# Pooling output projection: the twelve sums of weight blocks on GpSimd in place of VectorE

## The reference, cut to what matters

```python
def pooling_layer(x, g_norm, w_in, w_grp, b_grp, scale, w_out):
    ...
    mix = mix.reshape(B, S, POOL_WIDTH) * scale          # 256 x 4096
    return (mix * jax.nn.silu(z)) @ w_out                # w_out: 4096 x 2048
```

## Time and profile before

| | us |
|---|---|
| median of 3 runs | 2607.45 |
| lowest and highest | 2606.75, 2607.81 |
| the profiled execution's own time | 2608.36 |
| its span, first to last instruction | 2606.5 |
| TensorE busy, matmuls | 2590.2 (99%) |
| VectorE busy | 2058.8 (79%) |
| ScalarE busy | 1345.0 (52%) |
| GpSimd busy | 169.9 (7%) |

### The profile page before, as it was taken

The page is one execution under the profiler, slowest core; times in us unless marked ns, Lnnn a source line. Parts: engine busy times, 40 slices in busy tenths (PEclk is TensorE's granted clock), DMA queues, the critical chain, the costliest instruction groups (busy, mean ns, idle before and its releaser), DMA issues.

```text
span 2606.5 us, 35341 instructions
## 1 busy us (share of the span) xinstructions
PE 2590.2 (99%) x12626; PEld 2175.6 (83%) x12626; DVE 2058.8 (79%) x2881; ACT 1345.0 (52%) x1712; POOL 169.9 (7%) x332
## 2 busy tenths in 40 slices
PE   9999999999999999999999999999999999999998
PEld 7888888888888888888888888888888888788887
DVE  5887777776756868779877788987899899989565
ACT  5444444444444445444556555454656666574453
POOL 0000000000000000000002250432000000000000
PEclk9999999999999999999999999999999999999999
DMA  8555555555575565556565555645565565665754
GB/s 304 181 185 177 184 183 185 186 189 194 191 192 201 189 202 199 189 201 215 193 202 173 173 168 161 200 156 174 182 198 194 194 195 181 198 194 195 248 173 159
DMA packets 151494, 498.97 MB, mean 191 GB/s; under 512 B 28720, under 2 KB 29456, under 8 KB 150832
## 3 DMA queue, kind: packets, MB, share of 16 engines
q1 hardware_dynamic: 148736, 486.19, 56.4%
q0 software_dynamic: 2608, 10.74, 1.2%
HBM read 492.66 MB, written 4.21 MB: 191 GB/s over the span
## 4 chain that ended last, share of the span: by engine, by line
PE 97%; DVE 2%; ACT 1%; issue 0%; DMA 0%; POOL 0%; SPq 0%; DVEq 0%; ACTq 0%
PE PS L2246 23%; PE PS L2248 23%; PE PS L2247 23%; PE PS L2290 7%; PE PS L2269 5%; PE PS L2294 4%; PE PS L2274 2%; PE PS L2480 2%; PE PS L2461 2%; PE PS L2459 2%; PE PS L2460 2%; DVE yl L1938 1%; DVE wlo L1260 0%; PE PS L2487 0%; PE PS L2304 0%
## 5 line engine op out<-in xcount | busy, mean ns | idle before, releaser
L756 ACT CAST whi<-raw 128x1024 fp32r<-128x1024 f32 x887 | 928.0, 1050 | 1114.5 <-PE PS L2248 819.6
L1260 DVE TENSOR_TENSOR wlo<-raw,whi 128x1024 fp32r<-128x1024 f32 x887 | 1082.0, 1225 | 454.2 <-ACT whi L756 449.5
L2246 PE MATMUL PS<-whi,aHL 128*128 128x512 f32 x1904 | 744.7, 391 | 3.6 <-DVE wlo L1319 2.3
L2248 PE MATMUL PS<-whi,aHL 128*128 128x512 f32 x1904 | 741.1, 389 | 0.0
L2247 PE MATMUL PS<-wlo,aHL 128*128 128x512 f32 x1904 | 741.0, 389 | 0.0
L2246 PEld LDWEIGHTS PS<-whi,aHL 128*128 128x128 f32 x1904 | 357.5, 188 | 79.3 <-issue 2.7
L2248 PEld LDWEIGHTS PS<-whi,aHL 128*128 128x128 f32 x1904 | 357.4, 188 | 74.6
L2247 PEld LDWEIGHTS PS<-wlo,aHL 128*128 128x128 f32 x1904 | 357.6, 188 | 73.1
L2290 PE MATMUL PS<-aHL,whi 128*128 128x512 f32 x768 | 206.0, 400 | 1.7 <-DVE aHL L1296 1.4
L2290 PEld LDWEIGHTS PS<-aHL,whi 128*128 128x128 f32 x768 | 135.1, 190 | 24.5 <-DVE aHL L1296 1.6
L2269 PE MATMUL PS<-aHL,whi 128*128 128x512 f32 x512 | 128.2, 392 | 0.0
(11 more groups left out here) (395 smaller groups left out, 3112.3 us busy)
## 6 DMA issues: line engine op xcount, KB each, us to landing
raw<-in_stream SPq DMA_DIRECT2D x888, 512.0 KB, 3.3
quad<-in_stream SPq DMA_DIRECT2D x12, 512.0 KB, 5.6
xT<-in_xT SPq DMA_DIRECT2D x4, 512.0 KB, 6.7
H<-in_x SPq DMA_DIRECT2D x4, 512.0 KB, 8.5
pB<-in_pool_b POOLq DMA_DIRECT2D x4, 512.0 KB, 4.7
iT<-diag_in SPq DMA_DIRECT2D x16, 128.0 KB, 3.8
bg<-in_b_gate POOLq DMA_DIRECT2D x8, 256.0 KB, 3.8
out<-eb SPq DMA_DIRECT2D x8, 256.0 KB, 2.1
```

The costliest lines, as they stand in the source:

```text
L756: nc.scalar.copy(whi[:, s], raw[:, s]).then_inc(hi_done, 1 + blank)
L1260: nc.vector.tensor_tensor(wlo[:, s], raw[:, s], whi[:, s].bitcast(F32), ALU.subtract).then_inc(lo_done, 1 + blank)
L2246: mm(out, hi[:, kt + k, tok], whi[:, s, k], start=kt + k == 0, stop=False)
L2248: ins = mm(out, lo[:, kt + k, tok], whi[:, s, k], start=False, stop=last and k == KPC - 1)
```

## The change

The twelve sums are taken out of VectorE's `quad_lo` and made by GpSimd with the same operation on the same tiles, one group after the other, behind its two DMA issues. As the sum is no longer in the same queue as the low half that reads its place, GpSimd waits for that low half on `lo_done` (`low_taken`), and T3, which writes over 12, waits for T1, which reads it, and T4 for T2. SyncE gets one more wait: before it loads over the place of 21 it waits for the T4 sum, which reads 21.

```diff
@@ sync: loads of the next group @@
                     if w in ("T3", "22", "21", "T4") and g + 1 < len(PO_QUADS):
+                        if w == "21":
+                            sp.wait_ge(quad_add, added(g, "T4"))
                         sp.wait_ge(lo_done, q * RING + (RING + x - RING + 1))
                         quad_load(g + 1, {"T3": "11", "22": "12", "21": "22", "T4": "21"}[w])
@@ gpsimd @@
             pool.dma_start(pE[:], dram["pT"]).then_inc(row_in, 16)
+
+            def quad_sum(g, to, v):
+
+                loaded(pool, g, v)
+                nc.gpsimd.tensor_tensor(quad_at(g, to), quad_at(g, to), quad_at(g, v), ALU.add).then_inc(quad_add, 1)
+
+            def low_taken(g, w):
+
+                pool.wait_ge(lo_done, PO_AT + RING + PO_PLAN.index((g, w)) + 1)
+
+            for g in range(len(PO_QUADS)):
+                low_taken(g, "11")
+                quad_sum(g, "11", "12")
+                pool.wait_ge(quad_add, added(g, "T1"))
+                quad_sum(g, "12", "22")
+                low_taken(g, "T1")
+                quad_sum(g, "11", "22")
+                low_taken(g, "T2")
+                pool.wait_ge(quad_add, added(g, "T2"))
+                quad_sum(g, "11", "21")
             row_scale(M_FN)
@@ vector @@
-            def quad_sum(g, to, v, w):
-
-                loaded(dve, g, v)
-                nc.vector.tensor_tensor(quad_at(g, to), quad_at(g, to), quad_at(g, v), ALU.add).then_inc(quad_add, 1)
-
             def quad_lo(q, x, g, w):
...
-                if w == "11":
-                    quad_sum(g, "11", "12", "T1")
-                if w == "T1":
-                    dve.wait_ge(quad_add, added(g, "T1"))
-                    quad_sum(g, "12", "22", "T3")
-                    quad_sum(g, "11", "22", "T2")
-                if w == "T2":
-                    quad_sum(g, "11", "21", "T4")
```

## The result

| | before | after |
|---|---|---|
| median of 14 runs each, us | 2607.68 | 2612.08 |
| lowest and highest, us | 2606.75, 2608.71 | 2610.39, 2614.10 |
| profiled execution, own time, us | 2608.36 | 2610.59 |
| its span, us | 2606.5 | 2608.8 |

The change makes the kernel 4.4 us slower: ratio 1.0017, 95% interval 1.0009 to 1.0024. That is inside the 0.2% that was called no change, and clear of the measurement's own uncertainty. It lies within the stated range (2606.8 to 2614.5), 3.1 us above the likeliest time (2609.0), and just above the range given for that case alone (2607.5 to 2612).

What follows compares the result with a forecast made beforehand. TensorE, busy 2590.2 of 2606.5 us, was taken to bound the kernel. Gaps of 0.9 + 0.4 + 0.2 = 1.5 us in three groups, added to the median 2607.45, gave 2609.0 us, range 2606.8 to 2614.5.

Steps and rivals of the forecast that it cites:

- that case alone: Exclusion between GpSimd's sums and VectorE at 2.1 to 2.5 us: 2609.0 us, own range 2607.5 to 2612, chance 0.58.
- the relief: Twelve sums leaving VectorE free 13.6 us there, worth 0 us by itself since TensorE has no gap.
- exclusion in both directions: GpSimd's sums and VectorE's instructions with two SBUF inputs block each other; VectorE stands 2.0 us per sum where they meet.
- The replay: Step through three groups of sums and low halves, giving TensorE delays of 0.9, 0.4 and 0.2 us.
- the hold of a sum: One 1024-element sum on GpSimd takes 2.2 us: 0.2 start, 2.0 moving data and keeping VectorE out.
- the prediction's own rule: Three holds lie ahead of the first plain block after T2, so each extra 0.1 us costs 0.9 in all.
- the smallest margin: Block 21's low half in group 0 ends 1.4 us before TensorE asks for it, claimed as the least in hand.
- SyncE's loads: Quad loads at 1285.23 cost 0, at worst 1 us once; later by more than 2 us would show it wrong.
- The new wait: SyncE's wait for T4 before loading over block 21's place: cost 0, at worst 1 us once.
- No exclusion: Rival: the engines hardly exclude each other, VectorE's reads interleave and nothing starves; 2607.5 us, chance 0.20.
- The slow sum: Rival: a sum takes 3.3 us, delaying each group's first plain block after T2; 2618.9 us, chance 0.19.
- Faster: Rival: VectorE's freed 13.6 us let something start sooner; 2607 us at best, chance 0.03.

Runs made afterwards that it cites:

- e1: The twelve sums left out on any engine, products using unsummed blocks, against the kernel before: 2607.22 us, ratio 0.9999.
- f5: The change with only the three T4 sums on GpSimd, T1, T3 and T2 staying on VectorE: 2607.28 us, ratio 1.0000.
- e2: e1 plus twelve 128x1024 adds on GpSimd into unused tiles, which nobody waits for: 2611.31 us, ratio 1.0013.
- f8: The change once more, unaltered, for a second trace: 2611.25 us in one run.
- e3: e2 with three 128x1024 fills on GpSimd, which read nothing, in place of each add: 2607.62 us, ratio 1.0000.
- e4: The change with each sum made in two GpSimd instructions of 512 elements: 2609.80 us, ratio 1.0009.

## Why the prediction was right, and by how much it was off

**Right: the relief is worth nothing** (predicted 0; e1's window is the same to 0.01 us). TensorE was full, and VectorE's 13.6 us were cover, not path.

**Right: exclusion in both directions, and turns.** The replay named block 22 as the first victim, three holds deep, then block 26 by a little, block 44 behind the norm's row product, and group 2's first plain block, which is block 54. TensorE stopped before block 22, was 0.3 us late for block 26 and stopped before 44 and 54, and nowhere else in the stretch. That exclusion was taken from adds of 28 to 70 elements, and it held at 1024.

**Off: the size of one term, the hold of a sum.** I took 2.2 us for a sum, 2.0 of it on the port, from a slope over 8 to 76 elements. A sum that nobody delays takes 2.40 us (f5: mean 2401 ns), 0.2 of it start, so 2.2 on the port. This mis-sized term made the sum less than half of what came: 1.5 us forecast, 3.4 by the trace, 4.4 by the medians. By the prediction's own rule each 0.1 us costs 0.3 us a group, 0.9 in all: 1.5 + 2 x 0.9 = 3.3 us, and the trace has 3.4. That the total fits so well is partly luck. By groups the prediction had 0.9, 0.4 and 0.2, the corrected hold makes it 1.5, 1.0 and 0.8, and the trace has 1.8, 0.8 and 0.8, the last by a path that the replay did not have. The estimate halved from the Trainium skill (GPSIMD Engine Reference, section 3.1), 2.25 us, is hardly nearer than my 2.2, and short by 0.15.

**The third gap's path was not seen.** For group 2 the replay had block 54's low half between the sums T1 and T3, and took 0.2 us for a load that lands late. In the change T3's sum went first and the low half behind it. So the place was named for another reason than the one that came, which is luck. The reading that 1.4 us was the smallest margin was also wrong beyond group 0: before the change block 54's low half ended at 1297.73 and was asked for at 1298.58, 0.85 us in hand.

```profile
1296.50 1.23 DVE L1260 TENSOR_TENSOR wlo<-raw,whi 128x1024 fp32r<-128x1024 f32 x1 [2.38 <-ACT whi L756]
...
1298.58 0.39 PE L2459 MATMUL PS<-whi,oH 128*128 128x512 f32 x1
```

SyncE's loads were to come no more than 2 us later if the replay held, and they came 4.1 later. This sign against the prediction did show: 2.6 us of it are TensorE's delay, for which the replay had 1.3, and about 1.5 are T4's hold, which it did not carry on to the loads. The new wait itself cost 0, as said.

**Rivals.** No exclusion (0.20) is refuted by the low halves of 3.42 us and by e2. The slow sum (0.19) is not what happened: a sum alone takes 2.40 us, under the 2.6 that this rival asked for, and 3.44 only where it waits its turn. Faster (0.03) did not come.

**What stays open.** The delay by 1345 is 3.4 us, the medians differ by 4.4 (interval 2.3 to 6.3). The change's runs spread over 3.7 us, those of before over 2.0; its ten runs with a mean granted clock of 0.999 average 2611.6 us, the four with 0.997 or 0.998 2613.1. So part of the rest may go with the clock; where it dips in those runs no trace shows. The gap at 1371 that f8 has and the first trace has not adds another 0.7 us of scatter. What makes up the last 1.0 us of the 4.4 stays open. Whether VectorE's instructions with one input in PSUM are spared, as the replay assumed, was not tried: none of them met a sum.

## What to carry to other kernels

An add of two SBUF tiles that is moved from VectorE to GpSimd does not lie beside VectorE's instructions with two SBUF inputs: the move replaces 1.13 us of VectorE's time by a stop of up to 2.2. GpSimd work that only writes (e3) does lie beside them. Count the holds that can lie ahead of one urgent instruction, not the sums: three ahead of a plain block cost 1.3 us and more in group 0, two cost 0.3 us there and nothing in group 1, and one a group (f5) nothing. Look also at who is in the queue when a hold ends: where VectorE has nothing waiting, two sums run behind one another, and in group 2 the low half that came next stood behind the second. If the work must be moved, cut it up (which helped in two groups of three) or put it where no one is waiting, and look first whether VectorE is on the path at all.

## What the runs showed of the hardware that I had not expected

A recorded duration contains the wait for the other engine: one and the same 128x1024 subtraction shows 1.22, 1.73 and 3.42 us, one sum 2.40 and 3.44, and the idle time written beside them does not hold this wait. VectorE's busy time in this trace (2062.0 us) therefore says less than it seems about its work. After each gap of the stretch from 1209 to 1312 us, from 0.26 us (e4) to 1.69 (e2), the first matmul lasts 0.50 us instead of 0.39 at a granted clock of 1.00. The shift that a gap leaves (1.28 us at block 22) is larger than the idle time written beside it (0.98): idle is counted from the end of the last matmul, which lasts 0.39 us while matmuls start 0.23 apart, and block 22 itself takes 0.14 us longer than before (its first two matmuls start 0.34 apart).
